# A hybrid attention block: order of the pairs, grouping of fp32 products, and buffers of turned probabilities

## The reference

```python
h = rms_norm(x, norm_g)
qa, ka, va, za, qb, kb, vb, zb, ga, gb = split(h @ w_in)       # 1024 -> 5376
ya = swa_sink_attention(rope(qa), rope(ka), va, sinks) * silu(za)   # 8 heads, 2 kv heads, 2 chunks of 64
yb = chunked_relpos_attention(qb, kb, vb, rel_bias) * silu(zb)      # 8 heads, own chunk + 8 back
merged = sigmoid(ga + b0) * (ya @ w_br_a) + sigmoid(gb + b1) * (yb @ w_br_b)
return rms_norm(x + merged @ w_out, final_g)
```

## Time and profile before

| | us |
|---|---|
| median of 3 runs | 3287.7 |
| lowest, highest | 3285.98, 3288.65 |
| profiled execution | 3286.18 |
| its span, first to last instruction | 3284.3 |
| TensorE busy | 3219.8 |
| GpSimd, ScalarE, VectorE busy | 1464.6, 1397.6, 1354.1 |

### The profile page before, as it was taken

One profiled execution on the slowest core, in us unless ns is written; L12 is line 12 of the kernel. 1 busy time (PEld: TensorE's weight loads), 2 busy tenths in 40 slices (PEclk: granted clock), 3 DMA queues, 4 the chain that ended last, 5 costly groups with the idle time before them and its releaser, 6 DMA issues.

```text
span 3284.3 us, 48054 instructions
## 1 busy us (share of the span) xinstructions
PE 3219.8 (98%) x15992; PEld 2464.9 (75%) x15992; DVE 1354.1 (41%) x2936; ACT 1397.6 (43%) x2929; POOL 1464.6 (45%) x1217
## 2 busy tenths in 40 slices
PE   7999999999999999999999999999999999999998
PEld 6777877778777787777877778777787777877776
DVE  3562345513455134551345513455134551345422
ACT  4543444433445334453444534444344443435432
POOL 5434453344533455334453345533455334553244
PEclk9999999999999999999999999999999999999999
DMA  4222432224322243222532224322353223432233
GB/s 163 79 82 87 173 109 70 76 91 168 113 69 77 87 168 115 70 75 87 171 112 70 75 89 173 109 70 75 92 171 107 70 75 93 173 102 70 68 93 115
DMA packets 114554, 339.29 MB, mean 103 GB/s; under 512 B 17392, under 2 KB 33904, under 8 KB 112112
## 3 DMA queue, kind: packets, MB, share of 16 engines
q1 hardware_dynamic: 114288, 335.95, 31.9%
HBM read 316.23 MB, written 17.04 MB: 101 GB/s over the span
## 4 chain that ended last, share of the span: by engine, by line
PE 87%; DVE 6%; issue 4%; ACT 3%; POOL 0%; DMA 0%; ACTq 0%; DVEq 0%; SPq 0%; POOLq 0%
PE acc L972 15%; PE acc L974 15%; PE acc L973 15%; PE ps_pt L1036 6%; PE ps_o L1067 5%; PE sc L972 4%; PE sc L973 4%; PE sc L974 4%; PE sc L1016 3%; PE sc L914 2%; PE sc L916 2%; PE sc L915 2%; PE sc L1007 2%; DVE negm L1315 2%; DVE sc L1307 1%
## 5 line engine op out<-in xcount | busy, mean ns | idle before, releaser
L795 POOL TENSOR_TENSOR w_lo<-w_raw,w_hi 128x512 fp32r<-128x512 f32 x928 | 1209.5, 1311 | 1747.0 <-ACT w_hi L1111 1746.1
L972 PE MATMUL acc<-h_hi,w_hi 128*128 128x512 f32 x2432 | 1004.4, 413 | 0.0
L974 PE MATMUL acc<-h_hi,w_lo 128*128 128x512 f32 x2432 | 952.0, 391 | 0.0
L973 PE MATMUL acc<-h_lo,w_hi 128*128 128x512 f32 x2432 | 949.6, 390 | 0.0
L1111 ACT ACTIVATE w_hi<-w_raw 128x512 fp32r<-128x512 f32 x928 | 578.2, 625 | 435.7 <-DMA w_raw<-w 132.1
L972 PEld LDWEIGHTS acc<-h_hi,w_hi 128*128 128x128 f32 x2432 | 457.1, 188 | 132.4 <-issue 56.3
L974 PEld LDWEIGHTS acc<-h_hi,w_lo 128*128 128x128 f32 x2432 | 456.4, 188 | 101.1
L973 PEld LDWEIGHTS acc<-h_lo,w_hi 128*128 128x128 f32 x2432 | 458.6, 189 | 75.8
L1199 ACT ACTIVATE probs_b<-sc,negm 128x640 f32<-128x640 f32 x256 | 203.7, 796 | 363.7 <-DVE negm L1315 363.1
L1206 ACT ACTIVATE probs_t<-ps_pt 128x512 f32<-128x512 f32 (+1 forms) x272 | 154.6, 568 | 323.3 <-PE ps_pt L1036 323.3
L1342 DVE SCALAR_TENSOR_TENSOR z<-th,sc 128x512 f32<-128x512 f32 x64 | 43.9, 686 | 451.2 <-PE sc L974 451.2
(11 more groups left out here) (134 smaller groups left out, 3798.3 us busy)
## 6 DMA issues: line engine op xcount, KB each, us to landing
w_raw<-w SPq DMA_DIRECT2D x464, 512.0 KB, 3.6
rows<-x SPq DMA_DIRECT2D x36, 512.0 KB, 7.2
xt<-x_t SPq DMA_DIRECT2D x16, 1024.0 KB, 9.9
part<-den_rows SPq DMA_DIRECT2D x128, 128.0 KB, 3.9
out<-rows SPq DMA_DIRECT2D x32, 512.0 KB, 2.9
x_in<-x SPq DMA_DIRECT2D x28, 512.0 KB, 5.3
cs<-rope_tab SPq DMA_DIRECT2D x8, 512.0 KB, 4.2
den_rows<-rden_t SPq DMA_DIRECT2D x256, 1.0 KB
```

The lines of the kernel that those rows point to most:

```text
L795: pool.tensor_tensor(w_lo[n % 2][:, c], w_raw[n % 2][:, c], w_hi[n % 2][:, c].bitcast(FP32), ALU.subtract).then_inc(w_split, 1)
L972: pe.matmul(dst[:, :], hi, src_hi[:, k, :], start=begin, stop=False)
L973: pe.matmul(dst[:, :], hi, src_lo[:, k, :], start=False, stop=False)
L974: mm = pe.matmul(dst[:, :], lo, src_hi[:, k, :], start=False, stop=end)
```

## The change

- `ORDER` begins with a long pair: 4, 0, 5, 1, 6, 2, 7, 3; the last pair is a short one. The weight tiles are reordered to match. In the lead k4 and q4 come first, and the four long scores of pair 4 stand at the quarters 9, 12, 14 and 17 behind the `vt` tiles, each exponential after the quarter that follows the score.
- A long pair has two bursts: S0 S1 V0 V1 V2 before T6, and S2 S3 V3 V4 V5 V6 at its end. For that `probs_t` has six buffers. `B_OUT` changes: T5, T9 and T10 are now copied by VectorE, T6 and T7 by ScalarE.
- The last two exponentials of a short pair, X2 and X3, are done in its own beats, ahead of T1 and T2, not in the long pair's before it. Long scores S0 stand ahead of V0 V1, S2 one quarter later.
- `turn_v` is done with the second quarter of the first pair. `EARLY` is 2; the split steps are now steps of the plan.
- The two branches' halves in `br`, and the two gates, change places.
- To make room, `g_out` (the final norm's factor, 512 KB) shares the space of `gate` and `part` and is fetched again in every block, at quarter 24 of the output product.

```diff
-ORDER = [0, 4, 1, 5, 2, 6, 3, 7]
+ORDER = [4, 0, 5, 1, 6, 2, 7, 3]
...
 A_OUT = (0, 1, 1, 0)
-B_OUT = (1, 0, 0, 1, 0, 0, 1, 1, 0, 0, 0)
-RING = 4
+B_OUT = (1, 0, 0, 1, 0, 1, 0, 0, 0, 1, 1)
+RING = 6
...
-    names = "k0 q0 v0 k4 q4 z0 q1 z4 k5 q5 z1 q2 z5 k6 q6 z2 q3 z6 k7 q7 z3"
-    tiles = [("vt", kk) for kk in range(O_TILES)] + [(t[0], int(t[1])) for t in names.split()]
-    for d in range(AHEAD):
-        tiles += [("ga", d), ("gb", d)]
-        if d == 0:
-            tiles.append(("z", SETS - 1))
+    names = ("k4 q4 k0 q0 v0 z4 k5 q5 z0 q1 k6 z5 q6 k7 q2 z1 z6 q7 z2 ga0 q3 z7 gb0 z3 "
+             "ga1 gb1 ga2 gb2")
+    tiles = [("vt", kk) for kk in range(O_TILES)] + [(t[:-1], int(t[-1])) for t in names.split()]
...
+G_OUT_AT = 24
...
-A_BEATS = "T0 F G T1 F H D T2 V0 V1 S0 F E0 T3 F F C S1 V2 V3 F E1 F S2 F E2 F L F S3 F E3 F N"
-B_BEATS = "F T0 F G T1 F H D T2 F T3 F C V0 V1 S0 S1 T4 F E0 T5 F E1 T6 F T7 F L V2 V3 S2 S3 T8 F E2 T9 F T10 E3 F N V4 V5 V6"
+A_BEATS = "T0 X2 F G F T1 X3 F H D T2 S0 V0 V1 F E0 T3 F C S1 V2 V3 F E1 F F S2 F E2 L F S3 F E3 F N"
+B_BEATS = "F T0 F G T1 F H D T2 F T3 F C T4 F T5 F S0 S1 V0 V1 V2 T6 F E0 T7 F E1 L T8 F T9 F T10 F N S2 S3 V3 V4 V5 V6"
 BEATS_QUARTERS = 12
-EARLY = 1
+EARLY = 2
+FIRST_SCORES = (9, 12, 14, 17)
...
-    lead += [*tile("k", 0), [*q[0], ("rope_in_k", 0)], q[1], [("rope_k", 0), *q[2]], q[3],
-             [*v[0], ("rope_in", 0)], v[1], [("rope", 0), *v[2]], v[3], [("turn_v", 0), *k4[0]], *k4[1:], *tile("q", 4)]
+    lead += [*tile("k", 4), *q4, *k, [*q[0], ("rope_in_k", 0)], q[1], q[2], [("rope_k", 0), *q[3]],
+             [*v[0], ("rope_in", 0)], v[1], v[2], [("rope", 0), *v[3]]]
     for t in range(TT):
-        at_ = QUARTERS * O_TILES + 16 + t
-        lead[at_] = [("scores", 0, t), *lead[at_], ("exps", 0, t)]
+        at_ = QUARTERS * O_TILES + FIRST_SCORES[t]
+        lead[at_] = [("scores", ORDER[0], t), *lead[at_]]
+        lead[at_ + 1] = [*lead[at_ + 1], ("exps", ORDER[0], t)]
+    lead[-1] = [*lead[-1], ("keep_k", ORDER[0])]
+    for t in range(TT):
...
-    fill = tiles(("z", 0), ("gb", AHEAD - 1))
-    first_fill = TILES.index(("z", 0))
+    fill = tiles(("z", ORDER[0]), ("gb", AHEAD - 1))
+    first_fill = TILES.index(("z", ORDER[0]))
+    fill[1] = [("turn_v", 0), *fill[1]]
...
+            elif kind == "X":
+                plan.append(("exps", s, no))
+                if no == TT - 1 and s in KEPT:
+                    plan.append(("keep_k", s))
...
+            if at_ == G_OUT_AT:
+                plan.append(("fetch_g",))
             if kk == O_TILES - 1:
                 plan.append(("add_rows", half, c))
-    return plan
+
+    out = []
+    late = TILES.index(("ga", AHEAD)) if EARLY > 1 else None
+    for step in plan:
+        out.append(step)
+        if step[0] == "mm" and step[2] in SPLIT_AT and not (step[1] == late and step[2] < EARLY):
+            half = SPLIT_AT.index(step[2])
+            out.append(("split", step[1] + 2 - half, half))
+        if step == ("mm", TILES.index(("br", 0)), QUARTERS - 1) and late:
+            out.append(("split", late + 1, 1))
+    return out
...
-    probs_t = [at(f"probs_t{i}", [P, BLK], FP32, pt_at + 4 * BLK * i) for i in range(RING)]
-    pa_at = pt_at + 4 * BLK * RING
-    assert pa_at + 4 * TT * A_KEYS <= off[0]
+    probs_t = [at(f"probs_t{i}", [P, BLK], FP32, pt_at + 4 * BLK * i) for i in range(4)]
+    probs_t += [sb(f"probs_t{i}", [P, BLK]) for i in range(4, RING)]
+    pa_at = pt_at + 4 * BLK * 4
+    assert pa_at + 4 * TT * A_KEYS <= m_at + 8 * 4 * KT * BLK
...
-    g_out = sb("g_out", [P, D])
...
+    g_out = at("g_out", [P, D], FP32, gate_at)
...
+                    elif step[0] == "fetch_g":
+                        if last:
+                            sp.wait_ge(m_done, (b + 1) * KT)
+                        else:
+                            sp.wait_ge(rstd_turned, b + 2)
+                        sp.dma_start(g_out[:, :], final_g).then_inc(g_came, 16)
...
-                    pe.wait_ge(y_done, b * SETS + (POS[PAIRS - 1] + 1, SETS)[c // 2])
+                    pe.wait_ge(y_done, b * SETS + (POS[SETS - 1] + 1, SETS)[c // 2])
...
+                    row = (k + PAIRS) % SETS if branch else k
...
+                if t == 0:
+                    dve.wait_ge(g_came, 16 * (b + 1))
```

More of the change, by code:

```diff
@@ L154, in tiles @@
         return [g for t in TILES[TILES.index(first):TILES.index(last) + 1] for g in tile(*t)]
-    q, v, k4 = tile("q", 0), tile("v", 0), tile("k", 4)
+    q4, k, q, v = tile("q", 4), tile("k", 0), tile("q", 0), tile("v", 0)
     lead = [[("mm", n, c)] for n in range(O_TILES) for c in range(QUARTERS)]
@@ L233, in block_plan @@
                 elif c == 2 and d == 0:
-                    plan.append(("keep_v", SETS - 1))
+                    plan.append(("keep_v", ORDER[-1]))
     for e in range(KT):
@@ L334, in turn_table @@
             no[step[1:]] = (len(no), engine, on[engine])
-    assert len(no) % RING == 0
     return no, on
@@ L408, in program @@
     pt_at = m_at + 8 * TT * B_KEYS
-    probs_t = [at(f"probs_t{i}", [P, BLK], FP32, pt_at + 4 * BLK * i) for i in range(RING)]
-    pa_at = pt_at + 4 * BLK * RING
-    assert pa_at + 4 * TT * A_KEYS <= off[0]
+    probs_t = [at(f"probs_t{i}", [P, BLK], FP32, pt_at + 4 * BLK * i) for i in range(4)]
+    probs_t += [sb(f"probs_t{i}", [P, BLK]) for i in range(4, RING)]
+    pa_at = pt_at + 4 * BLK * 4
+    assert pa_at + 4 * TT * A_KEYS <= m_at + 8 * 4 * KT * BLK
     y_lo_at = y_at + 4 * SETS * BLK
-    pre = [at(f"pre{i}", [P, BLK], FP32, y_lo_at + 4 * BLK * n) for i, n in enumerate((3, 6))]
+    pre = [at(f"pre{i}", [P, BLK], FP32, y_lo_at + 4 * BLK * n) for i, n in enumerate((3, 2))]
     bias = sb("bias", [P, 9, A_KEYS])
@@ L419, in program @@
     g_in = sb("g_in", [P, KT])
-    g_out = sb("g_out", [P, D])
     cs = sb("cs", [P, 2, BLK])
     th = sb("th", [P, 2 * AHEAD, BLK])
-    gate = sb("gate", [P, BLK])
     part_at = off[0]
@@ L426, in program @@
     turned = at("turned", [P, BLK], FP32, part_at)
+    gate_at = off[0]
+    gate = sb("gate", [P, BLK])
     whole_at = off[0]
     whole = sb("whole", [P, BLK])
+    g_out = at("g_out", [P, D], FP32, gate_at)
     spread = at("spread", [P, TT, P], FP32, whole_at)
@@ L523, in program @@
     o_done = sem("o_done")
+    g_came = sem("g_came")
     out_sent = sem("out_sent")
@@ L527, in program @@
     c_dve = sem("c_dve")
-    N_CONSTS = 5
+    N_CONSTS = 4
     ADDED = HALVES * TT - O_BANKED
@@ L542, in half_tile @@
         return slice(half * (KT // 2) * P, (half + 1) * (KT // 2) * P)
-    def split_at(step):
-        half = SPLIT_AT.index(step[2])
-        return step[1] + 2 - half, half
     def wait_full(eng, b, step):
@@ L714, in _ @@
             load_w(0, 1)
-            for dst, src in ((g_out[:, :], final_g), (bias[:, 0:8, :], near), (far_sb[:, :], far),
+            for dst, src in ((bias[:, 0:8, :], near), (far_sb[:, :], far),
                              (sink_sb[:, :], sinks), (gb_raw[:, :], gate_b)):
@@ L807, in body @@
                 for step in PLAN:
-                    if step[0] == "mm" and step[2] in SPLIT_AT:
-                        n, half = split_at(step)
+                    if step[0] == "split":
+                        n, half = step[1:]
                         if not (last and n >= NW):
@@ L971, in products @@
                     end = k == KT - 1 or branch and k == 3
-                    pe.matmul(dst[:, :], hi, src_hi[:, k, :], start=begin, stop=False)
-                    pe.matmul(dst[:, :], hi, src_lo[:, k, :], start=False, stop=False)
-                    mm = pe.matmul(dst[:, :], lo, src_hi[:, k, :], start=False, stop=end)
+                    row = (k + PAIRS) % SETS if branch else k
+                    pe.matmul(dst[:, :], hi, src_hi[:, row, :], start=begin, stop=False)
+                    pe.matmul(dst[:, :], hi, src_lo[:, row, :], start=False, stop=False)
+                    mm = pe.matmul(dst[:, :], lo, src_hi[:, row, :], start=False, stop=end)
                 if end:
@@ L1174, in body @@
                     kind = step[0]
-                    if kind == "mm" and step[2] in SPLIT_AT:
-                        n, half = split_at(step)
+                    if kind == "split":
+                        n, half = step[1:]
                         if not (last and n >= NW):
@@ L1468 @@
     starts = {"qa": 0, "ka": 512, "va": 640, "za": 768, "qb": 1280, "kb": 1792, "vb": 2304, "zb": 2816,
-              "ga": 3328, "gb": 4352}
+              "ga": 4352, "gb": 3328}
     def columns(name, n):
@@ L1478, in columns @@
         return starts[name + "a"] + a_ch[n * P:(n + 1) * P]
-    branches = np.concatenate([w_br_a[0][a_ch], w_br_b[0]])
+    branches = np.concatenate([w_br_b[0], w_br_a[0][a_ch]])
     tiles = []
@@ L1508 @@
         "final_g": np.ascontiguousarray(np.broadcast_to(final_g, (P, D))),
-        "gate_b": np.ascontiguousarray(gate_bias[0].reshape(2 * KT, P).T),
```

(1 more changed line is left out.)

## The result

The changed kernel takes 3329.6 us (median; 3328.2 to 3331.0), the one before 3287.6: a ratio of 1.0125, 95% interval 1.0112 to 1.0138, 42 us slower. Forecast were 27 us (3314, own range 3300 to 3328). The profiled execution took 3329.2, its span is 3327.3.

The account below looks back on a forecast made before the run. TensorE, busy 98% of the span, was taken to bound the kernel. Terms of -2.4, -1.7 and +7.6 us gave +3.5 a block, +28 over eight, about 1 less for the first: 3314 us, range 3278 to 3334.

Parts of the forecast that it names:

- part 1: TensorE, fewer bursts and regrouped scores: fixed charges and a small wait saved, -2.4 us a block.
- The burst's 0.28: Long pair, two bursts instead of three: entry 0.09, value group 0.15, turn behind it 0.04; 1.1 us a block.
- part 2: TensorE waits that go, at the short values' turn, first pair's T1, lead's last scores and tail: -1.7 us a block.
- The tail: Last pair's `y_lo`: 2.0 us of wait before, 1.4 stays afterwards, so -0.6 a block.
- part 3: Waits that come, +7.6 us a block; long scores two quarters apart wait 1.1 in three short pairs and lead, +4.5.
- T8 and T4: Long-pair turns behind ScalarE's and VectorE's queues: T8 waits 0.45 in four pairs, +1.8; T4 0.35 in three, +1.0 a block.
- S0 and S1 of a short pair: S0 ahead of V0 V1, VectorE still busy: +0.1 us in each of three pairs, bounds 0 and 0.5 each.
- At nothing: Late exponentials X2, X3 and `g_out` fetched in each block: counted as no cost; fetch bounds 0 and 1 us a block.
- Rival 1: Score wait comes, turn waits do not, as jobs fall elsewhere on ScalarE and VectorE: 3292 us; chance 0.14.
- rival 2: S2 to S3 need not be 5.34 us apart, no score wait: 3255, or about 3278 with turn waits; chance 0.17.
- Rival 3: More collisions (X3 late, S0's shaping late for S1, weights late), 0.5 at some six places a block: 3338; chance 0.13.
- rival 4: No grouping charge on TensorE, a product's price is its columns alone, part 1 gives nothing: 3334 us; chance 0.04.

Follow-up runs that it names:

- three bursts: Kernel with the four edits, but long pairs in three bursts as before: 3322.2 us; with copies also shared as in the kernel before, 3269.4 us.
- four edits: Changed kernel with short-pair S2 earlier, lead scores at 9, 12, 15, 18, E0 ahead of a tile's last quarter, long-pair T3 copied by ScalarE: 3264.8 us together.

## Why the prediction was right, and where its sizes were off

**The direction and its cause** were right: the new waits outweigh what regrouping saves. By its steps:

- *Charges saved by regrouping (part 1).* The burst's 0.28 was measured as 0.20 to 0.28 in four long pairs. The short scores' 1.3 and the long scores' loss of 0.4 were not tried by themselves. TensorE's busy time fell by 8 us, but that is a modelled number. One slip of mine: before, T9 and T10 of the last pair stood side by side, and T10 right ahead of the burst, with no quarter between (the last two are empty). A turn with plain fp32 right behind it takes 0.44 instead of 0.47 (1712.09 to 1712.53 in the new lead), and no turn followed that burst; so about 0.1 a block of what I counted was never there to save.
- *Waits that go (part 2).* `turned` went as said. The tail was said to keep 1.4 and kept about 1.1 (0.94 in the row and 0.1 to 0.15 that it leaves out); taking it out alone gave 10 to 12 us, 1.3 to 1.5 a block. The wait of T1 behind a z tile stayed, as said (0.9 in the row).
- *Long scores two quarters apart (part 3).* 1.1 in three short pairs and once in the lead, as said: 5.33 to 5.40 apart against 5.34 in the earlier trace rows, and worth 25.5 us in the short pairs alone where I priced 27.
- *T8 and T4.* T8 came 2.14 to 2.22 after T7 (2.2 forecast), T4 2.17 after T3 in three pairs of four (2.18 forecast). The sharing of T3 was worth 7.3 us (8 forecast).
- *S0 and S1 of a short pair:* the term that was mis-sized most. I gave 0.1 with a bound of 0.5, and looked at VectorE only. It is 0.5 in all three pairs (S0 to S1 6.19 to 6.26, where 5.71 is work), and from ScalarE: E0 stands behind quarter 4, which ends a tile, the same queue that I had priced for T8 in the same sum. That is +1.2 a block. The prediction named a wait from S0's place as a sign against itself; it came.
- *The lead's S3:* not in the sum at all, 0.9 a block. Again exponentials behind the end of a tile. With S1 it is 2.1 a block, 17 us, and the forecast was 15 us short.
- *At nothing.* X2, X3 and the fetch of `g_out` indeed show no wait of their own: T1 and T2 of a short pair start with no idle time ahead of them.

With these the parts give -2.3, -2.0 and 7.6 + 2.1 = +9.7, together +5.4 a block. The trace says what a block gained: from the transposes of `spread` in one block to those in the next (and from the last to the end) seven stretches are 5.3 to 7.5 longer, 6.0 in the mean, and the first, which holds block 1's pairs, only 0.5. Block ends are some 0.3 longer, with as much scatter in either kernel, and their cause was not tried; where the rest lies is open.

Part of the nearness of 27 to 42 is luck: two misses had opposite signs. The later blocks were forecast 2.5 too small each, and the first 2.0 too large. I took 1 off for its shorter scores. In fact its long scores wait more than later ones (10.2 us in the rows, 6.6 in the second block), but the kernel before waited there as well (4.9 us, no such row in later blocks), and none of the turns of its long pairs waits. The measured time lies within the stated range of 3278 to 3334 and 2 us above the forecast's own.

**The rivals.** Rival 1 (turn waits do not come) and rival 2 (no score wait) fall by the rows above. Rival 3 (more collisions, 3338) and rival 4 (no charge to save, 3334) were both nearer in time than the forecast. Of rival 3's collisions one came, S1 late, at the place it named but by ScalarE and not by VectorE's shaping. Rival 4 falls by the 0.20 to 0.28 of the burst, whatever its time. Its rule is the one that the prediction took from the Trainium skill ("FP8 and Floating Point Precision", section TensorE Precision Notes): four passes through the array for true fp32. That rule leaves out the charge for the group, and the measurement decides for the rows; no run here tells whether the 0.43 us for each 128 columns is four passes.

## What to carry to other kernels

The one charge that was tried, a burst, came out as the price list said; but the new order lost more than twice its savings (9.7 against 4.3 us a block, by the sum above) in waits which could be read from the same trace: before moving a step, take the least distance seen between dependent steps (here 5.3 us from score to score) and compare it with the work the new order leaves between them, at every place where the pattern occurs. For a step that waits on an engine's result, write down that engine's whole queue ahead of it; a step put behind the end of a tile in that queue waits for the tile's job, whatever its own input does. And a choice of engine for copies belongs to one order of steps: with a sharing made for two bursts, three bursts looked 53 us worse than they are.

## What the hardware showed

- A turn right after a burst, entering a burst and the group of values each have a fixed charge on TensorE, 0.04, 0.09 and 0.15 us by the earlier trace rows (the 0.04 rests on an estimate), and their sum was found again: one burst less took 0.20 to 0.28 off in four long pairs, 26.24 instead of 26.52 in one.
- Waits on TensorE in one block added up almost without loss: four edits alone 67.2 us, together 64.8.
- 512 KB more of DMA in a block, and SyncE's queue held until it landed (3.9 us in the median), could not be seen in the time (3329.9 against 3329.6).
